# Summing the residual and all expert outputs in PSUM through a mixture-of-experts stage

## The chip, the cores and the metric

The kernel runs on one core of one Trainium2 chip. Its time is the device time of one execution in microseconds. Before the change the median of 3 runs was 1287.55 us (1286.89 to 1288.41).

## The reference

A decoder block on 256 tokens of width 1024, all in float32. The input goes through an RMSNorm, three token mixers (RWKV-7, windowed attention, cross-attention), a gated merge and an output projection, and is added to the residual `h`. Then 32 experts follow, of which each token takes four:

```
def clamped_swiglu(h):
    h_glu, h_lin = h[..., ::2], h[..., 1::2]
    h_glu = jnp.minimum(h_glu, SWIGLU_LIMIT)
    h_lin = jnp.clip(h_lin, -SWIGLU_LIMIT, SWIGLU_LIMIT)
    return h_glu * jax.nn.sigmoid(SWIGLU_ALPHA * h_glu) * (h_lin + 1.0)

top_vals, top_idx = lax.top_k(xt @ w_router + b_router, 4)
gates = jax.nn.softmax(top_vals, axis=-1)
# for each expert e on its tokens:
y = clamped_swiglu(xt[tok] @ w1[e] + b1[e]) @ w2[e] + b2[e]      # w1: 1024 x 2048, w2: 1024 x 1024
h = h + (sum over the 4 chosen experts of gate * y)
out = rms_norm(h, final_norm_w)
```

The weights of one expert are 12.58 MB, those of all 32 are 402.7 MB. Every expert is computed, each on at most 64 tokens; further passes run only if an expert has more tokens.

## The kernel before

There is no scheduler: each engine has its own hand-written program, and semaphores order them. The first 365 us hold the mixers and the router. The rest is the expert stage, which works on pairs of experts, 16 pairs in all. TensorE's program for the pair of experts E and E+1 (`pair`, L1058) is:

- `up(E)`: the first layer, 8 steps `c`, each with four 64-column matmuls of 512 columns into PSUM banks 0 and 1. The weights of a step lie in one slot of a ring. After each step `slots_used` is incremented.
- `down(E-1)`: the second layer of the expert before, 4 steps of the same sort into bank 3.
- `turn(E)`: four transposes of the activations into bank 2.
- `up(E+1)`, with pieces of other work put between its steps by `between(c)` (L1072): after step 0 the transposed gates of the last pair (`turn_gates`, bank 6), after steps 2 and 5 the `scatter` of the last pair's outputs to token rows, into banks 6 and 7 for the first 128 tokens and then the same banks for the second 128.
- `gather(N+1)` (L970): 16 matmuls that pick the next pair's tokens, into banks 4 and 5; then `down(E)` and `turn(E+1)`.

VectorE does the SwiGLU (`swiglu`, L1747: two additions of the bias out of banks 0 and 1, two clamps, two products), then multiplies the gathered tokens by the norm weight out of PSUM into `xg` (`gathered`, L1707), and adds each scattered half to the residual rows `xrows` in SBUF (`add_up`, L1768: 1024 columns at a time). ScalarE does the sigmoid and copies the transposes and the second layer's outputs out of PSUM.

In the first pair `up(0)` is followed by `second_bias(0)` (L1048): two matmuls of the gates of all experts (32 rows) by their second biases into banks 6 and 7, which VectorE adds to `xrows`; `second_bias(1)` stands after step 3 of `up(1)`.

SyncE issues the weight loads, each of 2 MB (two slots) or 1 MB, in the order of use. The ring holds 18 slots of 1 MB. A load for a pair of slots waits until `slots_used` says that TensorE has finished the slots' former content (`free`), so two steps of `up` or `down` set off one load.

At the end (`one_pass`, L1099) the last `down` goes into bank 4. The last two scatters go into banks 6, 7 and 0, 1, VectorE adds them to `xrows` in four pieces of 512 columns (`add_halves`, L1775), ScalarE sums the squares of each piece out of `xrows`, and VectorE scales `xrows` into `outrow` (L1842), which is stored.

Of the kernel before, what the change touches and what calls it, by code (L numbers as in the profile page):

```python
# [16 lines left out]
P = 128  # L17
# [128 lines left out]
def build(nc, x, mem, w_in, rwkv_w2, rwkv_a2, rwkv_g2, swa_sinks, w_mem_kv, w_gate, w_branch, w_out,  # L146
# [12 lines left out]
    with ExitStack() as ctx:  # L159
# [323 lines left out]
        def _(pe):  # L483
# [486 lines left out]
            def gather(N):  # L970

                pe.wait_ge(sel_sb, N + 2)
                for c in range(KC):
                    for t in range(TT):
                        last = mm(ps[:, 4 + c // 4, (c % 4) * P:(c % 4 + 1) * P], hn[:, t, c * P:(c + 1) * P],
                                  sel[:, t, :, :], c % 4 == 0 and t == 0, t == 1)
                last.then_inc(xg_ps, 1)
# [46 lines left out]
            def turn_gates(N, first):  # L1024

                pe.wait_ge(selg_sb, N + 1)
                if first:
                    pe.wait_ge(b2_sb, 2)
                else:
                    pe.wait_ge(acc_sb, N * 2)  # L1030
                for t in range(TT):
                    last = pe.transpose(ps[:, 6, t * P:(t + 1) * P], selg[:, t, :, :].rearrange("p e s -> p (e s)"), ident)  # L1032
                last.then_inc(selgT_ps, 1)

            def scatter(N, t, bank=6, halves=False):
# [4 lines left out]
                elif bank == 6:  # L1040
                    pe.wait_ge(acc_sb, N * 2 + 1)
# [4 lines left out]
                last.then_inc(sc_ps, 1)  # L1046

            def second_bias(t):  # L1048
# [3 lines left out]
                else:  # L1052
                    pe.wait_ge(b2_sb, 1)
                for n in range(2):
                    last = mm(ps[:, 6 + n, :], gatesT[0:NE, t * P:(t + 1) * P], b2rows[0:NE, n * 512:(n + 1) * 512])
                last.then_inc(b2_ps, 1)

            def pair(q, a, p, first, last, turn_wait=None):  # L1058

                E, N, r = q * NE + a * GROUP + 2 * p, q * NPAIR + a * (GROUP // 2) + p, 2 * p  # L1060
                very_first, second = turn_wait == "first", turn_wait == "second"
# [5 lines left out]
                if very_first:  # L1067
                    second_bias(0)
                else:
                    turn(E)  # L1070

                def between(c):  # L1072
                    if first:
                        if very_first and c == 0:
                            turn(E)
                        elif very_first and c == 3:
                            second_bias(1)
                    elif c == 0:
                        turn_gates(N - 1, second)
                    elif c == 2:  # L1080
                        scatter(N - 1, 0)
                    elif c == 5:
# [4 lines left out]
                def turns(i):  # L1087
                    if i == 2:
                        turn(E + 1)
                        turn_gates(N, False)  # L1090
# [3 lines left out]
                else:  # L1094
                    gather(N + 1)
                    down(q, a, r, E, 0 if very_first else 4, False, None, very_first)
                    turn(E + 1)

            def one_pass(q, very_first=False):  # L1099
                N0 = q * NPAIR  # L1100
                if not very_first:
                    pe.wait_ge(acc_sb, N0 * 2)
                if not very_first:
                    gather(N0)
                pair(q, 0, 0, True, False, "first" if very_first else None)
                pair(q, 0, 1, False, False, "second" if very_first else None)
# [4 lines left out]
                pair(q, GROUPS, 0, False, True)  # L1111
                down(q, GROUPS, 1, q * NE + NE - 1, 0, True)
                scatter(N0 + NPAIR - 1, 0, 6, True)
                scatter(N0 + NPAIR - 1, 1, 0, True)
# [9 lines left out]
        def _(act):  # L1124
# [237 lines left out]
            def gates_turned(N):  # L1362
                act.wait_ge(selgT_ps, N + 1)
                act.activation(selgT.rearrange("p t n -> p (t n)"), ps[:, 6, 0:T], ACT.Copy).then_inc(selgT_sb, 1)
# [21 lines left out]
            def one_pass(q, very_first=False):  # L1386
# [7 lines left out]
                downed(q * NE + NE - 1, 1, 4, (0,) if very_first else (0, 1))  # L1394

                for t in range(TT):
                    act.wait_ge(acc_half, q * TT + t + 1)
# [475 lines left out]
```

## Time and profile before

| | |
|---|---|
| median of 3 runs | 1287.55 us (1286.89 to 1288.41) |
| the profiled execution's own time | 1288.56 us |
| its span in the profile | 1286.3 us |
| TensorE matmul busy | 1211.1 us (94%), 6550 instructions |
| VectorE busy | 370.6 us (29%) |
| ScalarE busy | 184.7 us (14%) |
| TensorE's granted clock, mean | 0.998 |
| bytes read from HBM | 447.48 MB, 349 GB/s over the span |
| chain that ended last | PE 63%, DMA 31%, DVE 4% |

The profile shows one execution. PE is TensorE's matmuls, PEld its weight loads, DVE VectorE, ACT ScalarE, SP SyncE; a q behind a name is the engine's instruction queue. A float32 matmul is two records in the trace, so a count x4 of matmuls is two matmuls of the program. The 1.0 to 2.3 us between the span and the run's own time lie outside what the engines record.

### The profile page before, as it was taken

Reading aid. Unit: us, or ns where it says so; the run is one execution under the profiler, and the core shown is the slowest. Engines: PE = TensorE matmul, PEld = TensorE weight load, DVE = VectorE, ACT = ScalarE, POOL = GpSimd, SP = SyncE. Lnnn points to the kernel's source line nnn. Section 1 sums busy time; section 2 is a strip of 40 time slices with the busy share of each in tenths; the row PEclk is TensorE's granted clock in tenths of the full one; section 3 lists DMA queues with packets and bytes.
Section 4 is the critical chain, followed back from the end, with each engine's and each line's share of the span. In section 5 each row is a group of like instructions: output and inputs, shape, how many; then the busy total and the mean of one; then the engine's idle time right before and its main releaser. Section 6 shows DMA issues by size and latency. Waiting matters only on the chain.

```text
span 1286.3 us, 15495 instructions
## 1 busy us (share of the span) xinstructions
PE 1211.1 (94%) x6550; PEld 591.9 (46%) x6550; DVE 370.6 (29%) x629; ACT 184.7 (14%) x357; POOL 0.2 (0%) x4
## 2 busy tenths in 40 slices
PE   9999999999999999999998989898998989898986
PEld 7886788888543333333332323232333323232322
DVE  2158452411142233131331313122223313131223
ACT  2225521200120000100011000000010010100002
POOL 0000000000000000000000000000000000000000
PEclk9999999999999999999999999999999999999999
DMA  9354212695489999999999999999999999999995
GB/s 360 108 170 132 66 35 67 213 396 217 150 297 418 429 428 427 428 426 428 426 429 425 431 427 430 428 427 431 425 431 425 431 425 431 427 429 430 426 427 212
DMA packets 52131, 449.26 MB, mean 349 GB/s; under 512 B 5584, under 2 KB 18000, under 8 KB 26864
## 3 DMA queue, kind: packets, MB, share of 16 engines
q1 hardware_dynamic: 51744, 447.49, 84.3%
q10 hardware_dynamic: 336, 1.05, 0.3%
q8 instruction: 37, 0.61, 0.2%
q14 instruction: 14, 0.11, 0.0%
HBM read 447.48 MB, written 1.05 MB: 349 GB/s over the span
## 4 chain that ended last, share of the span: by engine, by line
PE 63%; DMA 31%; DVE 4%; issue 1%; ACT 1%; SPq 0%; DVEq 0%; PEldq 0%; ACTq 0%
PE ps L485 62%; DMA ring<-in_w_exp 19%; DMA upper<-in_w_exp 11%; PE ps L1021 1%; DVE ring L1485 1%; PE ps L746 0%; DMA xrows<-in_x 0%; DVE ring L1588 0%; DVE upper L1569 0%; ACT ring L1131 0%; DVE ring L1482 0%; PE ps L1032 0%; PE ps L652 0%; DVE upper L1524 0%; ACT upper L1197 0%
## 5 line engine op out<-in xcount | busy, mean ns | idle before, releaser
L485 PE MATMUL ps<-ring,upper 128*64 128x512 f32 (+4 forms) x2688 | 516.5, 527 | 30.6 <-DMA ring<-in_w_exp 26.3
L485 PE MATMUL ps<-upper 128*64 128x512 f32 (+5 forms) x1836 | 329.2, 461 | 23.4 <-DMA upper<-in_w_exp 15.8
L485 PEld LDWEIGHTS ps<-ring,upper 128*64 128x64 f32 (+2 forms) x2688 | 165.4, 136 | 340.3 <-issue 295.1
L485 PEld LDWEIGHTS ps<-upper 128*64 128x64 f32 (+3 forms) x1836 | 152.3, 154 | 191.4 <-issue 161.0
L485 PE MATMUL ps<-xT,ring 128*128 128x256 f32 x672 | 150.5, 381 | 0.4 <-DVE xT L1446 0.4
L485 PEld LDWEIGHTS ps<-xT,ring 128*128 128x128 f32 x672 | 126.1, 190 | 18.7 <-issue 1.1
L1752 DVE TENSOR_TENSOR upper<-ps,merged 128x512 f32<-128x512 f32 x32 | 22.1, 692 | 352.6 <-PEq L995 352.6
L1773 DVE TENSOR_TENSOR xrows<-xrows,ps 128x1024 f32<-128x1024 f32 x30 | 36.6, 1222 | 296.6 <-PE ps L485 296.6
L1349 ACT ACTIVATE xT<-upper 128x512 f32<-128x512 f32 x32 | 20.2, 631 | 544.9 <-DVE upper L1755 544.9
L1355 ACT ACTIVATE factors<-ps 64x512 f32<-64x512 f32 x63 | 37.3, 592 | 238.5 <-PEq L1016 237.7
L485 PE MATMUL ps<-factors,cst 128*128 128x512 f32 x128 | 63.2, 617 | 1.0 <-DVE factors L1832 1.0
L485 PE MATMUL ps<-upper,ring 128*128 128x256 f32 (+1 forms) x272 | 55.5, 364 | 0.3 <-DVE merged L1605 0.3
L485 PEld LDWEIGHTS ps<-upper,ring 128*128 128x128 f32 (+1 forms) x272 | 44.8, 189 | 9.6 <-issue 3.7
L1745 DVE STREAM_SHUFFLE merged<-merged 128x1024 f32<-128x1024 f32 x32 | 43.2, 1350 | 0.0
L485 PEld LDWEIGHTS ps<-factors,cst 128*128 128x128 f32 x128 | 21.8, 189 | 43.2 <-issue 43.2
L1765 DVE TENSOR_TENSOR xT<-upper,xT 128x512 f32<-128x512 f32 x32 | 34.2, 1067 | 1.1
L1021 PEld LDWEIGHTS ps<-cst,xT 128*128 128x128 f32 x128 | 13.4, 140 | 35.8 <-issue 35.0
L1021 PE MATMUL ps<-cst,xT 128*128 128x128 f32 x128 | 20.7, 284 | 8.0 <-PE ps L485 7.7
L485 PE MATMUL ps<-ring,merged 128*128 128x512 f32 x64 | 28.3, 595 | 0.0
L1607 DVE TENSOR_TENSOR upper<-upper,ps 128x512 f32<-128x512 f32 x8 | 5.5, 688 | 68.3 <-PE ps L485 68.3
L1760 DVE SCALAR_TENSOR_TENSOR upper<-upper 128x512 f32<-128x512 f32 x32 | 22.2, 692 | 1.1
L1711 DVE TENSOR_TENSOR upper<-ps,prm 128x512 f32<-128x512 f32 x32 | 20.7, 687 | 4.6 <-PE ps L485 4.4
(227 smaller groups left out, 491.8 us busy)
## 6 DMA issues: line engine op xcount, KB each, us to landing
ring<-in_w_exp SPq DMA_DIRECT2D x124, 2048.0 KB, 37.3
upper<-in_w_exp SPq DMA_DIRECT2D x63, 2048.0 KB, 37.3
ring<-in_w_exp SPq DMA_DIRECT2D x10, 1024.0 KB, 36.5
ring<-in_w_gate SPq DMA_DIRECT2D x9, 1024.0 KB, 5.2
ring<-in_w_in SPq DMA_DIRECT2D x8, 896.0 KB, 12.0
ring<-in_w_in SPq DMA_DIRECT2D x8, 640.0 KB, 4.0
ring<-in_w_branch SPq DMA_DIRECT2D x5, 1024.0 KB, 5.1
ring<-in_w_mem_kv SPq DMA_DIRECT2D x4, 1024.0 KB, 5.0
```

The costliest lines, as they stand in the source:

```text
L485: return pe.matmul(o, l, r, start=start, stop=stop, skip_group_check=True)
L1021: last = pe.transpose(ps[:, 2, m * P:(m + 1) * P], act_[:, m * P:(m + 1) * P], ident)
L1349: act.activation(sig, glu, ACT.Sigmoid, scale=ALPHA).then_inc(sig_sb, 1)
L1355: act.activation(yrow[64 * parity:64 * parity + 64, dh * 512:(dh + 1) * 512], ps[64 * dh:64 * dh + 64, bank, :], ACT.Copy).then_inc(yrow_s ...
L1485: link(dve.reciprocal(pinc, pinc))
L1607: link(TTn(gsig[:, m % 2, :], gsig[:, m % 2, :], ps[:, 7, :], ALU.mult))
L1711: TTn(xg[:, 4 * b:4 * b + 4, :], ps[:, 4 + b, :].rearrange("p (c s) -> p c s", c=4), prm[:, PCOLS["ffnp"] + 4 * b:PCOLS["ffnp"] + 4 * b + ...
L1745: dve.stream_shuffle(b1all, b1rows, [e] * NE).then_inc(b1_spread, 1)
L1752: TTn(glu, ps[:, 0, :], b1all[:, 0:D:2], ALU.add).then_inc(glu_raw, 1)
L1760: STT(lin, lin, 1.0, glu, ALU.add, ALU.mult).then_inc(prod_sb, 1)
L1765: TTn(act_.rearrange("p (c q) -> p q c", c=4), lin.rearrange("p (q c) -> p q c", c=4), sig.rearrange("p (q c) -> p q c", c=4), ALU.mult).t ...
L1773: TTn(a, a, ps[:, 6:8, :], ALU.add).then_inc(acc_sb, 1)
```

## The change

The final sum is no longer kept in `xrows` in SBUF. Banks 4 to 7 hold it from the first pair on: `residual(t)` multiplies the residual rows by an identity matrix into two banks and adds the second-bias product to them without clearing, and each later scatter adds to the same banks. VectorE's additions (`add_up`, `add_halves`, `second_bias`) are gone. The other users of banks 4 to 7 move: the gather goes to banks 3 and 2, which `down` and `turn` use; the gates' transposes go to bank 2; the last `down` goes to bank 0. For this the waits change: `gather` waits until ScalarE has copied bank 2, `down` waits for the first half of `gathered`, `turn` for the second. The two halves of `gathered` are placed inside the SwiGLU of the pair's second expert. At the end ScalarE and VectorE read the sum straight out of banks 4 to 7.

```diff
@@ gather, down (TensorE)
-                        last = mm(ps[:, 4 + c // 4, ...], hn[:, t, c * P:(c + 1) * P],
+                        last = mm(ps[:, 3 - c // 4, ...], hn[:, t, c * P:(c + 1) * P],
                                   sel[:, t, :, :], c % 4 == 0 and t == 0, t == 1)
-                last.then_inc(xg_ps, 1)
+                    if c % 4 == 3:
+                        last.then_inc(xg_ps, 1)
...
-            def down(q, a, r, E, whole=4, final=False, between=None, very_first=False):
+            def down(q, a, r, E, whole=4, final=False, between=None, very_first=False, gathered=None):
                 pe.wait_ge(actT_sb, E + 1)
-                bank, hidden = (4, act_last) if final else (3, actT)
+                if gathered is not None:
+                    pe.wait_ge(xg_sb, gathered * 2 + 1)
+                bank, hidden = (0, act_last) if final else (3, actT)
@@ scatter, residual (TensorE)
-                    last = mm(ps[:, bank + n, :], selgT[:, t, :], yrow[:, n * 512:(n + 1) * 512])
+                    last = mm(ps[:, 4 + 2 * t + n, :], selgT[:, t, :], yrow[:, n * 512:(n + 1) * 512], False)
...
-            def second_bias(t):
+            def residual(t):
                 if t == 0:
                     pe.wait_ge(gT_sb, 1)
-                else:
-                    pe.wait_ge(b2_sb, 1)
+                    pe.wait_ge(xg_sb, 2)
                 for n in range(2):
-                    last = mm(ps[:, 6 + n, :], gatesT[0:NE, t * P:(t + 1) * P], b2rows[0:NE, ...])
-                last.then_inc(b2_ps, 1)
+                    mm(ps[:, 4 + 2 * t + n, :], ident, xrows[:, t, n * 512:(n + 1) * 512])
+                    mm(ps[:, 4 + 2 * t + n, :], gatesT[0:NE, t * P:(t + 1) * P], b2rows[0:NE, ...], False)
@@ pair (TensorE)
-                if very_first:
-                    second_bias(0)
-                else:
+                if not very_first:
                     turn(E)
                 def between(c):
                     if first:
-                        if very_first and c == 0:
+                        if very_first and c == 1:
                             turn(E)
-                        elif very_first and c == 3:
-                            second_bias(1)
-                    elif c == 0:
-                        turn_gates(N - 1, second)
-                    elif c == 2:
+                        elif very_first and c in (3, 6):
+                            residual(c // 5)
+                    elif c == 1:
+                        turn_gates(N - 1, E)
+                    elif c == 3:
                         scatter(N - 1, 0)
-                    elif c == 5:
+                    elif c == 6:
                         scatter(N - 1, 1)
...
                 else:
+                    pe.wait_ge(actT_sb, E + 1)
                     gather(N + 1)
-                    down(q, a, r, E, 0 if very_first else 4, False, None, very_first)
+                    down(q, a, r, E, 0 if very_first else 4, False, None, very_first, N + 1)
+                    pe.wait_ge(xg_sb, N * 2 + 4)
                     turn(E + 1)
@@ the end (ScalarE)
-                    act.wait_ge(acc_half, q * TT + t + 1)
-                    act.activation(outrow[:, t, 0:512], xrows[:, t, 0:512], ACT.Square, ...)
+                    act.wait_ge(sc_half, q * TT + t + 1)
+                    act.activation(outrow[:, t, 0:512], ps[:, 4 + 2 * t, :], ACT.Square, ...)
@@ swiglu, pair, the end (VectorE)
                 TS(glu, glu, LIMIT, None, ALU.min).then_inc(glu_sb, 1)
+                if following is not None:
+                    gathered(following, 0, 3)
...
                 STT(lin, lin, 1.0, glu, ALU.add, ALU.mult).then_inc(prod_sb, 1)
+                if following is not None:
+                    gathered(following, 1, 2)
...
-                if not first:
-                    add_up(N - 1, 0, second)
-                    add_up(N - 1, 1)
-                swiglu(E + 1)
-                if not last:
-                    gathered(N + 1)
+                swiglu(E + 1, False, None if last else N + 1)
...
-                add_halves(q, N, 0, 6)
-                add_halves(q, N, 1, 0)
-                        STT(outrow[:, t, half], xrows[:, t, half], ss[:, 4 + t:5 + t], finw[:, half], ALU.mult, ALU.mult)
+                        STT(outrow[:, t, half], ps[:, 4 + 2 * t + b, :], ss[:, 4 + t:5 + t], finw[:, half], ALU.mult, ALU.mult)
```

TensorE in the first pair, from the second half of `up(0)` to the end of `up(1)`, before the change (`upper` and `ring` hold weights and activations, `cst` the identity and the gates, `ps` is PSUM; here one matmul is one count):

```order
L485 MATMUL ps<-upper 64x512 x8
L485 MATMUL ps<-upper,cst 128x512 x2
L485 MATMUL ps<-upper 64x512 x4
L1021 MATMUL ps<-cst,xT 128x128 x4
L485 MATMUL ps<-upper 64x512 x12
L485 MATMUL ps<-upper,cst 128x512 x2
L485 MATMUL ps<-ring,upper 64x512 x16
```

The same place after the change, from `turn(0)` (L1024) to the end of `up(1)`:

```order
L1024 MATMUL ps<-cst,xT 128x128 x4
L485 MATMUL ps<-upper 64x512 x8
L485 MATMUL ps<-xrows,cst 128x512
L485 MATMUL ps<-upper,cst 128x512
L485 MATMUL ps<-xrows,cst 128x512
L485 MATMUL ps<-upper,cst 128x512
L485 MATMUL ps<-ring,upper 64x512 x12
L485 MATMUL ps<-xrows,cst 128x512
L485 MATMUL ps<-upper,cst 128x512
L485 MATMUL ps<-xrows,cst 128x512
L485 MATMUL ps<-upper,cst 128x512
L485 MATMUL ps<-ring,upper 64x512 x4
```

The two bias matmuls between `up(0)` and `up(1)` are gone from there; four identity matmuls are new, and with the four bias matmuls they stand in two blocks inside `up(1)`.

VectorE in a middle pair, from the additions of the scatters to the gathered tokens, before:

```order
L1773 TENSOR_TENSOR xrows<-xrows,ps 128x1024 x2
L1752 TENSOR_TENSOR upper<-ps,merged 128x512
L1753 TENSOR_TENSOR upper<-ps,merged 128x512
L1755 TENSOR_SCALAR upper<-upper 128x512
L1757 TENSOR_SCALAR upper<-upper 128x512
L1760 SCALAR_TENSOR_TENSOR upper<-upper 128x512
L1765 TENSOR_TENSOR xT<-upper,xT 128x128x4
L1711 TENSOR_TENSOR upper<-ps,prm 128x512 x2
```

and after, where L1707 is `gathered` and L1749 to L1766 the SwiGLU:

```order
L1749 TENSOR_TENSOR upper<-ps,merged 128x512
L1750 TENSOR_TENSOR upper<-ps,merged 128x512
L1752 TENSOR_SCALAR upper<-upper 128x512
L1707 TENSOR_TENSOR upper<-ps,prm 128x512
L1756 TENSOR_SCALAR upper<-upper 128x512
L1759 SCALAR_TENSOR_TENSOR upper<-upper 128x512
L1707 TENSOR_TENSOR upper<-ps,prm 128x512
L1766 TENSOR_TENSOR xT<-upper,xT 128x128x4
```

The two wide additions are gone, and the two products of the gathered tokens stand ahead of the last product of the SwiGLU.

## Rows read from the trace of the kernel before

**Rows 1.** The page's 40 slices of the span: DMA busy tenths, and GB/s.
```profile
DMA  9354212695489999999999999999999999999995
GB/s 360 108 170 132 66 35 67 213 396 217 150 297 418 429 428 427 428 426 428 426 429 425 431 427 430 428 427 431 425 431 425 431 425 431 427 429 430 426 427 212
```

**Rows 2.** The chain that ended last, in order of time: start us, us, what.
```profile
453.18 10.85 PE ps L485 x64
...
506.88 10.85 PE ps L485 x64
...
711.70 15.17 PE ps L485 x56
...
770.44 15.18 PE ps L485 x56
...
1235.89 35.62 DMA ring<-in_w_exp
```

**Rows 3.** Timeline of SyncE's queue, 395 to 409 us: start, duration, the load issued.
```profile
395.75 0.33 SPq L445 DMA_DIRECT2D ring<-in_w_exp  x1
...
399.35 15.86 SPq L430 DMA_DIRECT2D ring<-in_w_exp  x4
...
406.91 0.33 SPq L430 DMA_DIRECT2D ring<-in_w_exp  x1
```

**Rows 4.** Loads issued at 302, 312, 395.75, 399.35, 406.91 us: us to landing last.
```profile
upper<-in_w_exp SPq DMA_DIRECT2D x1, 2048.0 KB, 7.2
...
upper<-in_w_exp SPq DMA_DIRECT2D x1, 2048.0 KB, 8.4
...
ring<-in_w_exp SPq DMA_DIRECT2D x1, 2048.0 KB, 11.1
...
ring<-in_w_exp SPq DMA_DIRECT2D x1, 2048.0 KB, 12.3
...
ring<-in_w_exp SPq DMA_DIRECT2D x1, 2048.0 KB, 9.8
```

**Rows 5.** Timeline of the first pair: start, duration, what [idle before it].
```profile
380.58 0.68 DVE L1753 TENSOR_TENSOR upper<-ps,merged 128x512 f32<-128x512 f32 x1
...
381.88 2.02 PE L485 MATMUL ps<-upper 128*64 128x512 f32 x8
...
384.43 5.62 PE L485 MATMUL ps<-upper 128*64 128x512 f32 x24
...
389.98 1.98 PE L485 MATMUL ps<-upper,cst 32*128 32x512 f32 x4
...
391.89 7.42 PE L485 MATMUL ps<-ring,upper 128*64 128x512 f32 x32
```

**Rows 6.** The same timeline from the end of `up(1)` to `turn(1)`.
```profile
399.51 0.69 DVE L1752 TENSOR_TENSOR upper<-ps,merged 128x512 f32<-128x512 f32 x1 [6.29 <-PEq L995]
...
402.23 1.07 DVE L1765 TENSOR_TENSOR xT<-upper,xT 128x512 f32<-128x512 f32 x1
403.21 7.09 PE L485 MATMUL ps<-ring,upper 128*64 128x512 f32 x32
...
410.46 0.63 PE L1021 MATMUL ps<-cst,xT 128*128 128x128 f32 x4 [0.16 <-PE ps L485]
```

**Rows 7.** Timeline of the end of the kernel.
```profile
1274.47 3.67 PE L485 MATMUL ps<-factors,cst 128*128 128x512 f32 x8 [0.98 <-DVE factors L1832]
...
1275.61 0.69 DVE L1784 TENSOR_TENSOR xrows<-xrows,ps 128x512 f32<-128x512 f32 x1 [1.28 <-PE ps L485]
...
1276.33 0.63 ACT L1398 ACTIVATE upper<-xrows 128x512 f32<-128x512 f32 x1 [2.11 <-DVE xrows L1784]
...
1280.83 1.42 DVE L1842 SCALAR_TENSOR_TENSOR upper<-xrows,ss,xT 128x512 f32<-128x512 f32 x2
```

**Rows 8.** The page: VectorE's additions of the scattered rows; the loads' median to landing.
```profile
L1773 DVE TENSOR_TENSOR xrows<-xrows,ps 128x1024 f32<-128x1024 f32 x30 | 36.6, 1222 | 296.6 <-PE ps L485 296.6
...
ring<-in_w_exp SPq DMA_DIRECT2D x124, 2048.0 KB, 37.3
```

More of the change, by code:

```diff
@@ L1022, in turn, with turn_gates, scatter @@
                 last.then_inc(actT_ps, 1)
-            def turn_gates(N, first):
+            def turn_gates(N, E):
                 pe.wait_ge(selg_sb, N + 1)
-                if first:
-                    pe.wait_ge(b2_sb, 2)
-                else:
-                    pe.wait_ge(acc_sb, N * 2)
+                pe.wait_ge(actT_sb, E + 1)
                 for t in range(TT):
-                    last = pe.transpose(ps[:, 6, t * P:(t + 1) * P], selg[:, t, :, :].rearrange("p e s -> p (e s)"), ident)
+                    last = pe.transpose(ps[:, 2, t * P:(t + 1) * P], selg[:, t, :, :].rearrange("p e s -> p (e s)"), ident)
                 last.then_inc(selgT_ps, 1)
-            def scatter(N, t, bank=6, halves=False):
+            def scatter(N, t, halves=False):
                 if t == 0:
@@ L1101, in one_pass @@
                 if not very_first:
-                    pe.wait_ge(acc_sb, N0 * 2)
-                if not very_first:
                     gather(N0)
                 pair(q, 0, 0, True, False, "first" if very_first else None)
-                pair(q, 0, 1, False, False, "second" if very_first else None)
+                pair(q, 0, 1, False, False)
                 pair(q, 0, 2, False, False)
@@ L1705, in _, with gathered @@
                     .then_inc(sel_sb, 1)
-            def gathered(N, very_first=False):
-                for b in range(2):
-                    if b == 0 or very_first:
-                        dve.wait_ge(xg_ps, N + 1 + (b if very_first else 1))
-                    TTn(xg[:, 4 * b:4 * b + 4, :], ps[:, 4 + b, :].rearrange("p (c s) -> p c s", c=4),
-                        prm[:, PCOLS["ffnp"] + 4 * b:PCOLS["ffnp"] + 4 * b + 4].unsqueeze(2).to_broadcast([P, 4, P]), ALU.mult).then_inc(xg_sb, 1)
-            gathered(0, True)
+            def gathered(N, b, bank):
+                dve.wait_ge(xg_ps, N * 2 + b + 1)
+                TTn(xg[:, 4 * b:4 * b + 4, :], ps[:, bank, :].rearrange("p (c s) -> p c s", c=4),
+                    prm[:, PCOLS["ffnp"] + 4 * b:PCOLS["ffnp"] + 4 * b + 4].unsqueeze(2).to_broadcast([P, 4, P]), ALU.mult).then_inc(xg_sb, 1)
+            gathered(0, 0, 4)
+            gathered(0, 1, 5)
             dve.wait_ge(top_exp, 1)
@@ L1766, in swiglu @@
                     ALU.mult).then_inc(act_sb, 1)
-            def add_up(N, t, very_first=False):
-                dve.wait_ge(sc_ps, N * 2 + t + 1)
-                if not very_first:
-                    dve.wait_ge(acc_sb, N * 2 + t)
-                a = xrows[:, t, :].rearrange("p (b n) -> p b n", b=2)
-                TTn(a, a, ps[:, 6:8, :], ALU.add).then_inc(acc_sb, 1)
-            def add_halves(q, N, t, bank):
-                for b in range(2):
-                    half = slice(b * 512, (b + 1) * 512)
-                    if b == 0:
-                        dve.wait_ge(sc_half, q * TT + t + 1)
-                        dve.wait_ge(acc_sb, N * 2 + t)
-                    else:
-                        dve.wait_ge(sc_ps, N * 2 + t + 1)
-                    TTn(xrows[:, t, half], xrows[:, t, half], ps[:, bank + b, :], ALU.add).then_inc(acc_sb if b else acc_half, 1)
-            def second_bias(t):
-                dve.wait_ge(b2_ps, t + 1)
-                a = xrows[:, t, :].rearrange("p (b n) -> p b n", b=2)
-                TTn(a, a, ps[:, 6:8, :], ALU.add).then_inc(b2_sb, 1)
             def largest_count():
@@ L1822, in one_pass @@
                     select(q, 0, q * NPAIR)
-                    gathered(q * NPAIR)
+                    gathered(q * NPAIR, 0, 3)
+                    gathered(q * NPAIR, 1, 2)
                 pair(q, 0, True, False, very_first)
```

43 lines of the change are left out of this document (20 added, 23 removed).

## The prediction, made before the changed kernel ran

> **What bounds the kernel now.** Read the page's slices first [rows 1]. From the slice that begins at 418 us to the one that ends at 1254 us the DMA line says 9 and the rate is 425 to 431 GB/s (the slice before them has 418): the reader is to see a plateau that no slice leaves. The experts' 402.7 MB at 428 GB/s take 941 us. This stream is the bound, though the page also shows TensorE at 94%.
>
> Second, the chain in order of time [rows 2]. The step from one `up` to the same one a pair later is 506.88 - 453.18 = 53.7 us early on and 770.44 - 711.70 = 58.7 us later; two experts' weights, 25.17 MB at 428 GB/s, take 58.8 us. So TensorE runs at its own pace at first, on weights loaded ahead, and from about 680 us each pair waits for weights. The last DMA piece of the chain ends at 1235.89 + 35.62 = 1271.5 us, and some 13 us of tail follow. The end is therefore: the last landing, plus the tail. TensorE and VectorE work inside a late pair is covered by 58.7 - 53.7 = 5.0 us of slack. But a time at which the stream has nothing to do is never given back.
>
> Third, is there such a time, and where? SyncE issues a load when TensorE has used two slots, and after 18 slots at most it must wait. I compare issue and landing [rows 3, 4]. A 2 MB load that meets an idle stream lands after 7.2 us (the one issued at 302 us), of which 2 MB at 428 GB/s are 4.9 and the rest, 2.3, is fixed. Longer times are queueing, so each row gives the reserve in the stream: 11.1 - 7.2 = 3.9 us at 395.75, 5.1 at 399.35, and only 9.8 - 7.2 = 2.6 us at 406.91. Thus at the first pair the stream is nearly out of work: these three land at 406.85, 411.65 and 416.7, one transfer of 4.9 us after the other, and TensorE delivers free slots just in time. A delay of TensorE here by more than 2.6 us becomes a hole in the stream. Over the whole stage the median to landing is 37.3 us [rows 8], so later nothing of this size reaches the stream.
>
> **The change part by part.**
>
> VectorE's 30 additions of 1222 ns [rows 8] go, 36.6 us of busy time, and those of the first pair. They ran beside the first layer, on an engine 29% busy; no row shows TensorE waiting for them. Worth 0.
>
> The scatters, gates' transposes and gather have the same number and shape of matmuls; only the bank and the step after which they stand differ. Worth 0. Adding onto what a bank holds is not seen in these positions before, but `up` and `down` do it at each step at the same 0.225 us per record as their first.
>
> New waits. `gather` waits for ScalarE's copy of the last transposes, made during `up` steps before. `down` waits for the first half of `gathered`: VectorE starts at 399.51, 0.16 us after `up(1)` ends, needs about 1.6 us for two additions and a clamp (additions of 0.69 follow each other by 0.6), waits until about 401.5 for the first half of the gather (it takes 3.8 us in all), and is done by 402.2; `down` begins at 403.21 anyway [rows 6]. `turn` waits for the second half and the SwiGLU: gather's end at 403.2, 0.69 us for the second product, 1.07 for the last SwiGLU product, so 405.0 against 403.3 before; `turn` comes at 410.46 [rows 6]. Cover left: 5.5 us. Behind these two waits queue `down`'s loads' releases and the next `up`; neither is late. If the cover of `down` were gone, each pair would still have the 5.0 us of slack. Worth 0.
>
> The first pair of TensorE is where the sum changes [rows 5]. I rebuild it step by step. `up(1)` started at 381.88, after `second_bias(0)`; it may start when VectorE has read banks 0 and 1, 380.58 + 0.68 = 381.26, so at about 381.33 now: -0.55 us. A step of `up` is 8 records of 0.225 = 1.8 us, a change of tile shape costs 0.15 at entry (5.55 us for 24 records and the switch to the next group). `second_bias(1)` took 391.89 - 389.98 = 1.91 us: 4 records of 0.43 and 0.19 to leave its shape. The new `residual(t)` has 8 records, 3.44 us, but alternates 128-row and 32-row tiles: four changes of shape at 0.19, so 4.2 us. If those inner changes are free it is 3.44 + 0.19 = 3.63, the same as the 3.67 us of the scatter's 8 records [rows 7]. I take 4.2, because the row of the 32-row tile shows a change being paid, and keep 3.63 as the lower end. `up(1)` with all in it took 399.35 - 381.88 = 17.47 us; now 17.47 - 1.91 + 0.15 + 2 x 4.2 = 24.1 us, ending at 405.45 instead of 399.35: +6.1 us (+5.0 at the lower end).
>
> What this does to the loads. That of step 5 goes at 397.5 (1.8 later, inside its reserve of 3.9), that of step 7 at 405.45: 6.1 later against a reserve of 5.1, so 1.0 us late. The next, issued from `down(0)`, goes at 406.91 + 6.1 = 413.0 and lands at 420.2 instead of 416.7: 3.5 us late, which is the delay less the reserve of 2.6. Later loads have growing reserves (TensorE frees 25.17 MB per 53.7 us, 469 GB/s against 428), so the hole stays at 3.5 us and every later landing moves by it. Bounds: 2.4 us with the cheap `residual`; with 8.4 us as the idle-stream time of a load (the one issued at 312 us [rows 4]) 4.7 us. None at all only if the stream catches up, a rival below.
>
> The Trainium skill prices a DMA otherwise ("DMA: Bandwidth & Descriptors", section "Anatomy of one DMA — SWDGE (gpsimd) path"): a fixed 2.0 us plus bytes over 436 GB/s, an estimate of 6.8 us for 2 MB. The trace has 7.2 for it. By the page the reserve would be 3.0 and the hole 3.1 us.
>
> The tail [rows 7]. Before, the first square on ScalarE waits for VectorE's addition: 1276.33 against 1275.61, when the scatter's first half is there. Now it starts at about 1275.61: -0.7 us. The chain behind it is ScalarE's own, so all of it moves if nothing else is late: the scatter's four matmuls come 0.9 us apart and are done at 1278.1, before the squares that need the last two; VectorE's last pair of products, at 1280.83, moves to 1280.1, and VectorE has only the first pair, moved as well, ahead of it. From PSUM instead of SBUF I take the same durations: the addition out of PSUM takes 0.69 us, half of the 1.42 for two all-SBUF products is 0.71. Worth -0.7; bounds -0.9 and 0.
>
> A rule that speaks against this: the Trainium skill ("VectorE: DVE Perf Modes", section "The TRN2 errata — SBUF-src ops pay a fixed extra latency per instruction") gives VectorE 120 cycles of overhead out of PSUM and 58 out of SBUF, by its clock there 0.065 us more per product, so an estimate of -0.6 instead of -0.7. The two rows just read show no such difference.
>
> **Sum.** Against the profiled execution: last landing 1271.5 + 3.5, tail 0.7 shorter: span 1286.3 + 2.8 = 1289.1, own time 1288.56 + 2.8 = 1291.4. That execution is 1.0 us above the median of the runs, so from the median: 1287.55 + 2.8 = 1290.35 us, +0.22%. A difference within 0.2% (2.6 us) is no change that this kernel's measurement can tell, so the forecast stands just on the slower side of it.
>
> **Rivals.**
>
> The cheap residual: the inner tile changes cost nothing, `residual` is 3.63 us, the hole 2.4, the time 1287.55 + 2.4 - 0.7 = 1289.25. For it: the scatter's 8 equal records in 3.67. Against: the 0.19 after the bias matmuls.
>
> Not slower: the stream takes the delay without a hole, because its queue holds more than the landings suggest, and only the tail counts: 1287.55 - 0.7 = 1286.85. It decides if the reserve at 406.91 is over 6 us rather than 2.6. For it: a landing tells when the last part of a load is down, and not how much of the next one has moved by then. Against: the stream's rate in 386 to 418 us is already under its plateau [rows 1].
>
> Faster by a better stream: without VectorE's 36.6 us of additions in SBUF the loads run at 429 instead of 428 GB/s; 0.23% of 890 us is 2.1 us, so 1284.8 with the tail and 1286.9 + 1.4 with the hole. Against: rates of slices differ by 6 GB/s with no relation to the additions.
>
> Slower by more: the new waits bite. If `down` or `turn` waited more than 5.0 us in each pair, TensorE would be the bound; 1 us over it in each of about 11 late pairs is 11 us, 1301. Against: 5.5 us of cover at `turn` and none missing at `down`.
>
> Or the change does nothing at the tail, since ScalarE's chain is held by something else: 1287.55 + 3.5 = 1291.05.
>
> **How the numbers follow.** Forecast, with the dead tail as its upper part: 0.58 (own range 1289.6 to 1292.2). Cheap residual: 0.17. No hole: 0.12. Better stream: 0.06. Waits: 0.07. Slower by over 0.2% (above 1290.1): two thirds of the forecast, the waits, a little of the cheap case, together 0.50. Faster by over 0.2% (below 1285.0): the better stream and a rest, 0.07. Within: 0.43. The range 1286.8 to 1292.3 leaves out the waits, the best of the stream and a tail above 4.7 us of hole, under 2 in 10.
>
> **What would show it.** In the profile after: `up(1)` ends near 405.4, and its records show `residual` at 4.2 or 3.6 us each; the load out of `down(0)` is issued near 413.0 and lands 7.2 us later, and 2 us windows around 408 to 415 show DMA under 1; the last landing is near 1275.0; the first square starts 1.1 us after the last scatter begins; `down` and `turn` show no idle time behind VectorE. A last landing at 1271.5, or `down` waiting for VectorE, would prove me wrong.

## The result, and the profile after

The changed kernel takes 1291.54 us (median of 10 runs, 1291.02 to 1292.22) against 1288.08 us of the kernel before on the same chip (10 runs, 1286.89 to 1288.76). The ratio is 1.0029 with a 95% interval of 1.0020 to 1.0038, so the change costs 3.5 us (2.6 to 4.9 by the interval). The forecast was 1290.35 us, +2.8 us, with 0.50 on slower; of the 1.2 us between the two times 0.5 is the kernel before, which measured 1288.08 this time and not 1287.55.

The profiled execution has a span of 1289.3 us, 3.0 more than before. The page's slices of the changed kernel answer to [rows 1]:

```profile
DMA  9343211695488999999999999999999999999995
GB/s 359 108 169 131 66 35 67 219 397 208 157 295 356 429 429 428 426 427 429 426 427 428 429 429 429 428 429 428 427 429 429 427 430 429 427 430 428 428 427 238
```

The plateau is the same. Only the slice ahead of it, 387 to 419 us, has 356 GB/s where it had 418: 62 GB/s for 32 us are 2.0 MB, about one load that was not carried there (part of it is the shift of the slice's edges).

Next the timeline of TensorE and VectorE in the first pair, which answers to [rows 5] (start, duration, what, [idle before it]):

```profile
381.25 3.82 PE L485 MATMUL ps<-upper 128*64 128x512 f32 x16 [1.49 <-DVE upper L1750]
...
385.58 3.82 PE L485 MATMUL ps<-upper 128*64 128x512 f32 x16
...
389.33 1.12 PE L485 MATMUL ps<-xrows,cst 128*128 128x512 f32 x2
...
390.39 1.12 PE L485 MATMUL ps<-upper,cst 32*128 32x512 f32 x2
...
393.55 5.62 PE L485 MATMUL ps<-ring,upper 128*64 128x512 f32 x24
...
399.10 1.12 PE L485 MATMUL ps<-xrows,cst 128*128 128x512 f32 x2
...
403.31 2.02 PE L485 MATMUL ps<-ring,upper 128*64 128x512 f32 x8
```

`up(1)` starts at 381.25 behind VectorE's second addition, and each residual takes 393.55 - 389.33 = 4.22 us and 403.31 - 399.10 = 4.21 us. `up(1)` ends at 405.3 to 405.4, as forecast; before it was 399.35.

SyncE's queue in the changed kernel, answering to [rows 3]:

```profile
397.41 0.33 SPq L445 DMA_DIRECT2D ring<-in_w_exp  x1
...
405.37 16.16 SPq L430 DMA_DIRECT2D ring<-in_w_exp  x4
...
413.08 0.33 SPq L430 DMA_DIRECT2D ring<-in_w_exp  x1
```

and the time to landing of these three, in that order, answering to [rows 4]:

```profile
ring<-in_w_exp SPq DMA_DIRECT2D x1, 2048.0 KB, 9.5
...
ring<-in_w_exp SPq DMA_DIRECT2D x1, 2048.0 KB, 8.7
...
ring<-in_w_exp SPq DMA_DIRECT2D x1, 2048.0 KB, 7.5
```

The last number falls to 7.5 us, near the 7.2 us of a load that meets an idle stream [rows 4]. It lands at 413.08 + 7.5 = 420.6 instead of 406.91 + 9.8 = 416.7: 3.9 us late. The load ahead of it lands at 414.1 instead of 411.7, already 2.4 us late. The three loads behind land 3.8 to 3.9 us later than their partners of before.

That the stream is empty in between is seen directly in 2 us windows of the changed kernel (of each line the end is what counts here: the DMA engines' busy share, and GB/s):

```profile
404.00:406.00 2.00, 1.69 (x9) 0.53 (x6) 0.53 (x1) 0.00 (x0) 0.00 (x0) 1.00 0.33 139
406.00:408.00 2.00, 2.00 (x20) 2.00 (x20) 1.39 (x4) 0.63 (x1) 0.00 (x0) 1.00 0.94 254
...
412.00:414.00 2.00, 2.00 (x12) 0.72 (x10) 1.45 (x3) 0.00 (x0) 0.00 (x0) 1.00 0.04 16
414.00:416.00 2.00, 2.00 (x12) 0.57 (x8) 0.00 (x0) 0.00 (x0) 0.00 (x0) 1.00 0.95 287
```

and of the kernel before, where nothing of the kind stands:

```profile
404.00:406.00 2.00, 2.00 (x12) 0.72 (x10) 1.97 (x7) 0.00 (x0) 0.00 (x0) 1.00 0.95 393
...
412.00:414.00 2.00, 2.00 (x12) 0.69 (x10) 0.00 (x0) 0.27 (x1) 0.00 (x0) 1.00 0.97 401
```

So the hole has two parts, one ahead of the load of step 7 (2.4 us of delay) and one ahead of the load out of `down(0)` (1.5 us more).

The new waits, at the end of `up(1)` and after it, answering to [rows 6]:

```profile
405.47 0.69 DVE L1749 TENSOR_TENSOR upper<-ps,merged 128x512 f32<-128x512 f32 x1 [20.49 <-PEq L996]
...
407.70 0.69 DVE L1707 TENSOR_TENSOR upper<-ps,prm 128x512 f32<-128x512 f32 x1 [0.61 <-PE ps L485]
...
409.38 7.09 PE L485 MATMUL ps<-ring,upper 128*64 128x512 f32 x32
409.49 0.69 DVE L1707 TENSOR_TENSOR upper<-ps,prm 128x512 f32<-128x512 f32 x1
410.10 1.06 DVE L1766 TENSOR_TENSOR xT<-upper,xT 128x512 f32<-128x512 f32 x1
...
416.78 0.63 PE L1024 MATMUL ps<-cst,xT 128*128 128x128 f32 x4 [0.31 <-PE ps L485]
```

The first product out of `gathered` (L1707) is done at 408.4, 1 us before `down` begins behind the gather; the second and the SwiGLU's last product are done at 411.2, and `turn` comes at 416.8. TensorE never waits for VectorE here. What is felt is small: it stands idle 0.31 us before this `turn`, where it was 0.16 [rows 6], and the same 0.31 against 0.16 before the gather. Both places have one more semaphore to wait for now, though no run separates that from the rest of the edit.

The chain, early and late, answering to [rows 2] (start, us, what):

```profile
459.66 10.85 PE ps L485 x64
...
513.67 10.85 PE ps L485 x64
...
850.43 10.88 PE ps L485 x64
...
909.18 10.88 PE ps L485 x64
...
1275.28 1.96 PE ps L485 x8
```

A pair takes 54.0 us where TensorE sets the pace, 0.3 more than before, which are the two short gaps of 0.15 us; where the stream sets the pace it takes 58.75, as before, so the slack takes them in. The last eight records of `down(31)`, which wait for the last landing, start at 1275.28; before, by the same row of the chain, at 1271.56. That is 3.7 us.

It is not simply the hole of 3.9 carried to the end. At 441.1 us one load lands 5.8 us after its forerunner instead of 4.9, so the delay against the kernel before is 4.8 us there; later each trace has a few such late landings at loads of its own, and the difference goes to 5.3 and back to 3.6 us by 1061 us. The agreement of 3.7 with 3.9 is therefore good to about 1 us only. The last section returns to this.

The end, answering to [rows 7]:

```profile
1278.20 3.67 PE L485 MATMUL ps<-factors,cst 128*128 128x512 f32 x8 [0.98 <-DVE factors L1802]
1279.33 0.60 ACT L1396 ACTIVATE upper<-ps 128x512 f32<-128x512 f32 x1 [1.39 <-PE ps L485]
...
1283.69 1.41 DVE L1810 SCALAR_TENSOR_TENSOR upper<-ps,ss,xT 128x512 f32<-128x512 f32 x2
```

The first square starts 1.13 us after the scatter instead of 1.86. From the scatter's start to VectorE's last pair of products it is 5.49 us, before 1280.83 - 1274.47 = 6.36. From 1275.28 to the end of the span it is 14.0 us; before 14.7. So 3.7 later, 0.7 shorter, 3.0 in all.

### The profile page after: what moved, and what is told of

Its sections match the earlier page's. It is cut to its first block, busy times and chain, and to the rows that moved or that the text cites. A ratio compares the mean times of both kernels' runs of the same rounds, so it can differ in the third digit from the quotient of the medians.

```text
span 1289.3 us, 15466 instructions
## 1 busy us (share of the span) xinstructions
PE 1216.4 (94%) x6558; PEld 593.8 (46%) x6558; DVE 328.0 (25%) x593; ACT 184.4 (14%) x357; POOL 0.2 (0%) x4
## 4 chain that ended last, share of the span: by engine, by line
PE 65%; DMA 29%; DVE 4%; issue 1%; ACT 1%; SPq 0%; PEldq 0%; DVEq 0%; ACTq 0%
PE ps L485 63%; DMA ring<-in_w_exp 20%; DMA upper<-in_w_exp 9%; PE ps L1024 1%; DVE ring L1483 1%; PE ps L746 0%; DMA xrows<-in_x 0%; DVE ring L1586 0%; DVE upper L1567 0%; ACT ring L1129 0%; PE ps L1032 0%; DVE ring L1480 0%; PE ps L652 0%; DVE upper L1522 0%; ACT upper L1195 0%
## 5 line engine op out<-in xcount | busy, mean ns | idle before, releaser
L1749 DVE TENSOR_TENSOR upper<-ps,merged 128x512 f32<-128x512 f32 x32 | 22.1, 692 | 693.1 <-PEq L996 693.1
L1766 DVE TENSOR_TENSOR xT<-upper,xT 128x512 f32<-128x512 f32 x32 | 34.0, 1064 | 0.6
L1024 PEld LDWEIGHTS ps<-cst,xT 128*128 128x128 f32 x128 | 13.4, 140 | 37.4 <-issue 37.4
L1024 PE MATMUL ps<-cst,xT 128*128 128x128 f32 x128 | 20.7, 284 | 9.6 <-PE ps L485 9.6
L1707 DVE TENSOR_TENSOR upper<-ps,prm 128x512 f32<-128x512 f32 x32 | 22.1, 692 | 11.2 <-PE ps L485 10.7
L1750 DVE TENSOR_TENSOR upper<-ps,merged 128x512 f32<-128x512 f32 x32 | 21.8, 681 | 0.0
## 6 DMA issues: line engine op xcount, KB each, us to landing
ring<-in_w_exp SPq DMA_DIRECT2D x124, 2048.0 KB, 36.6
upper<-in_w_exp SPq DMA_DIRECT2D x63, 2048.0 KB, 36.6
ring<-in_w_exp SPq DMA_DIRECT2D x10, 1024.0 KB, 36.6
```

Of the source, the lines that this page charges most:

```text
L1024: last = pe.transpose(ps[:, 2, m * P:(m + 1) * P], act_[:, m * P:(m + 1) * P], ident)
L1707: TTn(xg[:, 4 * b:4 * b + 4, :], ps[:, bank, :].rearrange("p (c s) -> p c s", c=4), prm[:, PCOLS["ffnp"] + 4 * b:PCOLS["ffnp"] + 4 * b + 4 ...
L1749: TTn(glu, ps[:, 0, :], b1all[:, 0:D:2], ALU.add).then_inc(glu_raw, 1)
L1750: TTn(lin, ps[:, 1, :], b1all[:, 1:D:2], ALU.add).then_inc(up_read, 1)
L1766: TTn(act_.rearrange("p (c q) -> p q c", c=4), lin.rearrange("p (q c) -> p q c", c=4), sig.rearrange("p (q c) -> p q c", c=4), ALU.mult).t ...
```

## The experiments

My theory: the two `residual` blocks delay TensorE's release of weight slots at the one place where the load stream has almost no work queued; the hole is the delay less the reserve, and later landings all move by it. Rival A: added TensorE work costs its time wherever it stands in the stage. Rival B: the new waits or the shared banks cost a little in every pair. Each run was timed beside the kernel before, and its ratio is to that.

**moved: the residual in the second pair.** The call goes from steps 3 and 6 of `up(1)` to the same steps of `up(2)`.

```diff
-                        elif very_first and c in (3, 6):
-                            residual(c // 5)
+                def second_pair(c):
+                    if c == 3:
+                        residual(0)
+                    elif c == 6:
+                        residual(1)
...
-                up(q, a, r, E, N, 0, turn_all_gates if very_first else None, first)
+                up(q, a, r, E, N, 0, turn_all_gates if very_first else second_pair if turn_wait == "second" else None, first)
...
```

> The changed kernel, with residual(0) and residual(1) moved from steps 3 and 6 of the first pair's up(1) to steps 3 and 6 of the second pair's up(2). All work is the same. My theory (the residual delays the slots that the load stream needs at a place where it has only 2.6 us of reserve, and later it has 8 us and more): no hole in the stream, up(1) ends near 396.8 us instead of 405.4, the load out of down(0) goes at about 404.3, the last landing comes near 1271.3, and only the shorter tail is left: 0.7 us under the kernel before, ratio 0.9994, that is 4 us faster than the changed kernel. Rival A (each us of added TensorE work costs a us wherever it stands in the stage): as the changed kernel, ratio 1.003. Rival B (the waits or the shared banks of every pair cost the time): as the changed kernel too, ratio 1.003.

Measured: 1288.45 us (11 runs, 1286.45 to 1290.55) against 1287.30, ratio 1.0006 (0.9997 to 1.0015). Most of the loss is gone with the same work in the program, so both rivals fall. It is 1.5 us above what I had expected, and the expected ratio, 0.9994, lies just outside the interval. Why stays open. The profiled execution is the slowest of the eleven, 2.1 us over the median, and its loads go 2.1 us later than in the other traces from 302 us on, before the changed part begins. In it the load of step 7 of `up(2)`, issued at 434.17 us,

```profile
upper<-in_w_exp SPq DMA_DIRECT2D x1, 2048.0 KB, 9.8
```

is left with a reserve of 2.6 us, and lands 6.1 us after the one ahead of it instead of 4.9. I had counted on 8 us of reserve and had not set against it the 8.4 us that the residual takes. But by my own theory 2.6 us left are no hole, and the stream does not run empty there: in 2 us windows from 438 to 444 us its busy share is 0.91 to 1.06, while the rate falls to 328 to 385 GB/s. The late landing is of the kind that the last section leaves open.

**twice: each residual done twice in the first pair.**

```diff
                         elif very_first and c in (3, 6):
                             residual(c // 5)
+                            residual(c // 5)
```

> The changed kernel with each residual done twice at its place in the first pair (the second time clears and sums again, so the result is the same): 8.4 us more TensorE work there. My theory: the reserve is used up already, so each us is a us: changed kernel + 8.4 us, about 1300 us, ratio 1.0094. Rival B (cost is in every pair): the first pair matters little, under 2 us more, since 5.0 us of slack in each late pair take it in; ratio 1.003 to 1.005. Rival A: 8.4 us more as well.

Measured: 1299.72 us (4 runs), ratio 1.0096 (1.0081 to 1.0112): 8.2 us over the changed kernel by the two medians, 9.0 if each is first taken against its own kernel before, for 8.4 us of work. The load out of `down(0)` goes at 421.50 and takes 7.5 us again, landing 8.4 us after that of the changed kernel. Once the reserve is gone, a microsecond is a microsecond, and the 5.0 us of slack in each later pair give none of it back. This trace also shows that the time of a load on an idle stream is not one number: the load of step 7 is issued at 413.79 us, 4.4 us after the one ahead of it has landed, and takes 8.4 us.

**grouped: the order inside the residual.**

```diff
                 for n in range(2):
                     mm(ps[:, 4 + 2 * t + n, :], ident, xrows[:, t, n * 512:(n + 1) * 512])
+                for n in range(2):
                     mm(ps[:, 4 + 2 * t + n, :], gatesT[0:NE, t * P:(t + 1) * P], b2rows[0:NE, n * 512:(n + 1) * 512], False)
```

> The changed kernel with the order inside residual(t) changed from identity, bias, identity, bias to identity, identity, bias, bias: two changes of tile shape inside or at the end instead of four. My theory: 0.38 us less in each residual (4.22 to 3.84 us), 0.8 us less delay, and the hole is 0.8 us smaller: ratio 1.0022. If the inner shape changes are not what makes four matmuls take 4.22 us, residual stays at 4.2 and the time at that of the changed kernel, ratio 1.0029.

Measured: 1290.80 us (9 runs), ratio 1.0026 (1.0016 to 1.0036). The ratios of this and of the changed kernel cannot be told apart; the traces can. TensorE's timeline of this kernel:

```profile
389.32 1.98 PE L485 MATMUL ps<-xrows,cst 128*128 128x512 f32 x4
391.23 1.98 PE L485 MATMUL ps<-upper,cst 32*128 32x512 f32 x4
393.14 5.62 PE L485 MATMUL ps<-ring,upper 128*64 128x512 f32 x24
```

The residual is 393.14 - 389.32 = 3.82 us instead of 4.22: each change of tile shape costs 0.2 us, as the forecast's working had it. The edit also parts the two matmuls that follow each other into one bank, but that is not the saving: in `dose_step6` below, ten identity matmuls into one bank take 8.85 us, 0.44 per record. `up(1)` ends at 404.5, 0.8 us earlier, and the load out of `down(0)` lands at 420.0, 0.6 earlier.

**tail_back: the end as before.** VectorE copies the finished banks to `xrows`, and the end reads `xrows`.

```diff
+                for t in range(TT):
+                    for b in range(2):
+                        half = slice(b * 512, (b + 1) * 512)
+                        dve.wait_ge(sc_ps if b else sc_half, q * TT + t + 1)
+                        dve.tensor_copy(xrows[:, t, half], ps[:, 4 + 2 * t + b, :]).then_inc(acc_sb if b else acc_half, 1)
...
```

> The changed kernel with the end as before: VectorE copies the four finished banks to xrows, ScalarE squares and VectorE scales out of xrows. My theory: the first square starts 0.7 us later behind the copy, the tail is 0.7 us longer, 1292.2 us, ratio 1.0034. Rival (the tail gave nothing, it is held elsewhere): as the changed kernel, 1.0029. The tail's own length in the trace, from the last scatter's start to the end of the span, tells it better than the ratio: 11.8 us against 11.1.

Measured: 1291.84 us (5 runs), ratio 1.0035 (1.0021 to 1.0049), too close to the changed kernel for the ratio. Its end in the timeline:

```profile
1278.04 3.67 PE L485 MATMUL ps<-factors,cst 128*128 128x512 f32 x8 [0.98 <-DVE factors L1802]
1279.17 0.69 DVE L1807 COPY xrows<-ps 128x512 f32<-128x512 f32 x1 [1.28 <-PE ps L485]
1279.89 0.63 ACT L1396 ACTIVATE upper<-xrows 128x512 f32<-128x512 f32 x1 [2.11 <-DVE xrows L1807]
...
1284.40 1.42 DVE L1815 SCALAR_TENSOR_TENSOR upper<-xrows,ss,xT 128x512 f32<-128x512 f32 x2
```

From the scatter to the last products it is 6.36 us, the very number of the kernel before, against 5.49 in the changed one. To the end of the span it is 11.7 against 11.1 us. The tail's gain, 0.6 to 0.9 us, is shown in the traces.

**third: the residual in the third pair.** Since banks 4 to 7 only add, the residual need not come first: the first pair's scatters clear the banks, and the residual is added in `up(4)`, where the reserve is larger.

```diff
-                    last = mm(ps[:, 4 + 2 * t + n, :], selgT[:, t, :], yrow[:, n * 512:(n + 1) * 512], False)
+                    last = mm(ps[:, 4 + 2 * t + n, :], selgT[:, t, :], yrow[:, n * 512:(n + 1) * 512], opens)
...
-                    mm(ps[:, 4 + 2 * t + n, :], ident, xrows[:, t, n * 512:(n + 1) * 512])
+                    mm(ps[:, 4 + 2 * t + n, :], ident, xrows[:, t, n * 512:(n + 1) * 512], False)
...
-                        scatter(N - 1, 0)
+                        scatter(N - 1, 0, False, turn_wait == "second")
...
```

> The changed kernel, but the first pair's scatters open banks 4 to 7 (they clear), and residual(0) and residual(1) are added without clearing in the third pair, after steps 3 and 6 of up(4); the sum is the same. My theory: the stream has about 12 us of reserve there against 8.4 us of added work, so neither the first pair nor this one makes a hole; only the shorter tail is left, 0.7 us under the kernel before: ratio 0.9994, below the kernel with the residual in the second pair (1.0006), whose trace shows one load there with only 2.6 us of reserve. Rival (the cost sits in the steady pairs, or added TensorE work costs wherever it stands): 1.002 to 1.003.

Measured: 1286.71 us (11 runs, 1285.60 to 1289.65) against 1287.86, ratio 0.9995 (0.9986 to 1.0004). It has the lowest median of the three placements and its ratio is well below the changed kernel's interval. Against the kernel before, the interval still holds 1; the 0.6 us that the ratio names fit the tail's 0.7, but are not clear of noise by the time alone. No load of its trace up to 500 us takes under 11.3 us to landing once the stream is full.

**dose_first: 9 us of dummy work in the first pair of third.** The result is the same, since step 0 clears.

```diff
-                    for z in range(2):
-                        for hf in range(2):
+                    for z, hf in [(z, hf) for z in range(2) for hf in range(2)] * (6 if c == 0 and more else 1):
...
```

> The kernel with the residual in the third pair, and with the four matmuls of step 0 of up(1) in the first pair done six times instead of once (each time they clear and write the same): 20 matmuls more, 9.0 us, nothing else. My theory: the reserve at the load out of down(0) is now the 2.6 us of before plus the 2.5 us that the bias matmuls and their wait took, so the hole is 9.0 - 5.1 = 3.9 us: kernel third + 3.9 us, ratio 1.0025 over before. Rival (the hole of the changed kernel came from the identity matmuls as such, their reads of xrows or their bank writes): no cost at all, ratio as third.

Measured: 1293.01 us (5 runs), ratio 1.0041 (1.0027 to 1.0055): 6.3 us over third, not 3.9. There is a cost though not one identity matmul was added, so these as such are not to blame; but my number was wrong. I had read the reserve at the load out of `down(0)`, while work at step 0 delays first the load of step 1. In third that load takes 11.3 us to landing, a reserve of 4.1; here it is issued 8.8 us later and takes

```profile
upper<-in_w_exp SPq DMA_DIRECT2D x1, 2048.0 KB, 7.3
```

and lands at 401.5 instead of 396.6: 4.9 us late, where 8.8 less 4.1 is 4.7. In 2 us windows from 390 to 394 us the stream moves nothing at all. The rest arises at the next two loads, which land 5.6 and 6.1 us after their forerunners though the stream had work (busy share 0.95 and more from 398 us on): 1.9 us that I cannot explain (see the last section).

**dose_step6: the same dose where the second residual stood.**

```diff
                         if very_first and c == 1:
                             turn(E)
+                        elif very_first and c == 6:
+                            for _ in range(10):
+                                mm(ps[:, 6, :], ident, xrows[:, 0, 0:512])
```

> The kernel with the residual in the third pair, and with ten matmuls of the identity by 512 columns of xrows into bank 6 (which is cleared and used for nothing until the second pair) after step 6 of up(1) in the first pair: 20 records of 0.43 us and the change of shape, 8.9 us, at the place where the changed kernel had its second residual. My theory, with the reserve now read at each load that the dose delays: in third the load of step 7 took 14.4 us to landing (reserve 7.2) and the one out of down(0) 11.6 us (reserve 4.4), so the hole is 8.9 - 4.4 = 4.5 us, third + 4.5 us, 1291.2 us, ratio 1.003, and the load out of down(0) lands at about 420.7. If the dose costs the same 6.3 us as the one at step 0 did, the reserve is not what decides; if it costs 8.9, there is no reserve.

Measured: 1291.43 us (10 runs, 1291.22 to 1291.85), ratio 1.0025 (1.0016 to 1.0035), 4.7 us over third by the medians, and 4.6 if each is taken against its own kernel before. The timeline has the dose, and the load out of `down(0)`, issued at 413.16, its time to landing:

```profile
394.62 8.85 PE L485 MATMUL ps<-xrows,cst 128*128 128x512 f32 x20
```

```profile
ring<-in_w_exp SPq DMA_DIRECT2D x1, 2048.0 KB, 7.6
```

It lands at 420.8; 420.7 was expected. The same 9 us cost 6.3 at one place and 4.7 at another of the same expert. The reserves there were nearly the same, 4.1 and 4.4 us; the difference is the unexplained part of `dose_first`.

**dose_loop: 36 us of dummy work in later pairs of third.** The edit is that of dose_first, on for the middle pair of each loop turn. The expectation below counts five turns and 45 us. There are four: `pe.Fori(1, GROUPS)` with `GROUPS = 5`, three pairs in each, three pairs ahead of the loop and one behind make the 16. The page agrees, with 6718 matmul records against the 6558 of third: 160 more, 36 us.

> The kernel with the residual in the third pair, and with the same 20 extra matmuls (9.0 us) in the second expert of the middle pair of each of the five loop turns: 45 us more TensorE work in all, in pairs 5, 8, 11, 14 and so on. My theory: the reserve there is 20 us and more, and three pairs give 15 us of slack, so nothing reaches the stream: time of third, within 1 us. Rival (TensorE work costs wherever it stands): + 45 us, ratio 1.035; a rival with the late pairs bound by TensorE in part: + 10 us or more.

Measured: 1286.55 us (11 runs), ratio 0.9992 (0.9983 to 1.0001): the extra work costs nothing that can be seen beside the 1286.71 of third. Of the page of this kernel, the busy times and the chain that ended last:

```profile
PE 1245.9 (97%) x6718; PEld 607.8 (47%) x6718; DVE 328.2 (26%) x593; ACT 184.5 (14%) x357; POOL 0.2 (0%) x4
...
PE 90%; DVE 4%; DMA 3%; issue 2%; ACT 1%; SPq 0%; PEldq 0%; DVEq 0%; ACTq 0%
```

The chain is 90% TensorE and 3% DMA, where that of the changed kernel is 65% and 29%, and yet not a microsecond is added. From 408 us on no load of this trace takes under 13.6 us to landing, so the stream never ran dry. This disposes of rival A in its pure form. It also warns of the chain's shares: they name TensorE here, although 36 us of its work are free.

**adds: VectorE's additions put back in third.** Two instructions of 1024 columns per pair, from the second pair on. They clear `xrows` before the third pair's residual reads it, so the residual is missing from this kernel's output; the instructions are the same.

```diff
+                if not first:
+                    for t in range(TT):
+                        TTn(xrows[:, t, :], xrows[:, t, :], xrows[:, t, :], ALU.subtract).then_inc(acc_sb, 1)
+                        dve.wait_ge(acc_sb, N * 2 + t - 1)
```

> The kernel with the residual in the third pair, and with two VectorE instructions of 1024 columns on xrows (which is no longer read) put back in each pair where the additions of the scatters stood, 30 in all, about 1.1 us each. My theory: time of third, within 1 us. Rival (the additions slowed the loads or the SwiGLU, so taking them away gained something that the hole hid): third + 2 us, ratio 1.001.

Measured: 1286.45 us (11 runs), ratio 0.9992 (0.9983 to 1.0001), the same as without them. The page has them at the weight of [rows 8]:

```profile
L1794 DVE TENSOR_TENSOR xrows<-xrows 128x1024 f32<-128x1024 f32 x30 | 36.6, 1219 | 0.5
```

36.6 us of VectorE work are worth nothing here, to within the 1 us or so of the intervals. They read SBUF only, not PSUM as the old ones did, so what reading PSUM may have cost is not tested by this run.

## Why the prediction was right

**The bound.** Last landing plus tail holds: 3.7 us on the one and -0.7 on the other are the 3.0 us of the span. (The tail of the kernel before is 1286.3 - 1271.5 = 14.8 us; the forecast's "some 13" was a slip without effect on its sum.)

**TensorE in the first pair.** Forecast: start of `up(1)` at 381.33, 4.2 us per residual, end at 405.45. Trace: 381.25, 4.22 and 4.21, 405.4. The choice of 4.2 over 3.63 was right, and `grouped` shows that the changes of tile shape are the difference.

**The hole.** Forecast 3.5 us, with the load out of `down(0)` going at 413.0 and landing at 420.2. Trace: 413.08 and 420.6, a hole of 3.9; the idle-stream time was 7.5 and not 7.2 us, which is 0.3 us of the 0.4 by which the term was too small. One step on the way there was wrong: the load of step 7 was to land 1.0 us late, 6.1 less a reserve of 5.1, and landed 2.4 us late, because it took 8.7 us and not 7.2 though the stream was all but empty (busy share 0.33 around its issue). A load that meets an idle stream took 7.2 to 8.7 us in these traces (8.4 to 8.7 for this one in the changed kernel, `twice`, `grouped`, `tail_back` and `dose_step6`), so a reserve read this way is uncertain by up to 1.5 us. The forecast had the 8.4 only as an upper bound for the load behind. That the step did no harm is luck: the load out of `down(0)`, which sets the hole, was issued by TensorE's progress and not by that landing, and took 7.5. The Trainium skill's estimate of 6.8 us for 2 MB ("DMA: Bandwidth & Descriptors", section "Anatomy of one DMA — SWDGE (gpsimd) path") would have given 3.1. The page fits it to loads issued from GpSimd, and these are issued from SyncE; with 7.3 to 7.6 us in three kernels the traces are 0.5 to 0.8 us above it, and up to 1.9 with the 8.7 just named.

**The tail.** Forecast -0.7, measured 0.7 in the span, and alone in `tail_back`. The Trainium skill's higher overhead of VectorE out of PSUM ("VectorE: DVE Perf Modes", section "The TRN2 errata — SBUF-src ops pay a fixed extra latency per instruction") is not seen: two products out of PSUM take 1.41 us, out of SBUF 1.42.

**What was priced at nothing.** The waits, the moved scatters and VectorE's additions: 0.15 us of idle TensorE before each gather and each second `turn`, hidden by the slack in later pairs and worth 0.15 us of the hole in the first; and `third`, which keeps all of them, is at 0.9995.

**The rivals.** The cheap residual, the lossless stream and the biting waits are excluded by the rows above. The better stream, priced at 2.1 us, is excluded by `adds` for work in SBUF. What is left between +2.8 and the measured +3.5 us is 0.4 of hole, and 0.3 within the noise of the runs and the late landings of about 1 us that all traces have. These also moved the last landing, so that its 3.7 us against the forecast's 3.5 is closer than the working deserves.

## What to carry to other kernels

Where a stream of loads is the bound, what the other engines did in these runs cost nothing until it emptied the stream's queue (36 us in `dose_loop`), and from there on it cost its full time for good (8.4 us in `twice`). So read, load by load, the time from issue to landing; less the time of a load that meets an idle stream, it is the reserve, and the least reserve among the loads that an edit delays decides. Take that time as a range from several loads, here 7.2 to 8.7 us, and look at the busy share in short windows to see whether the stream did run empty. Extra work goes to a place with reserve, and a sum in PSUM allows it, since its terms may come in any order as long as the first one clears.

## What the runs showed that I had not expected

The reserve differs between neighbouring loads: in third the load of step 7 of `up(1)` has 7.2 us and the next one, out of `down(0)`, 4.4. So work of one size has no one price. The same 9 us of TensorE work cost 6.3 us at step 0 of `up(1)`, 4.7 us at step 6, and nothing in each of four later pairs. Of the 6.3 us the reserve accounts for 4.7 to 4.9 only.

Landings of a full stream are 4.9 us apart, but now and then one comes 5.5 to 6.5 us after its forerunner. It is not wholly at random. The same load does it (5.7 to 5.8 us after the one ahead) in the changed kernel at 441.1 us, in `grouped`, `tail_back` and `dose_step6` near 441, and in `twice` at 449.6, and these are the five kernels whose stream had run dry in front of the load out of `down(0)`. The load of step 5 of `up(1)` does it in the kernel before (406.85), in `moved` (408.5) and in `dose_first` (413.2). What holds these loads up stays open; it is of the size of the tail's gain, and is why differences under 1 us are told here by the timelines and not by the ratios.
